# Where the fp32r operands of a 2048-wide two-block network lie modulo 256 bytes, on one core

## The reference

```
# first block
proj = rmsnorm(x) @ w_in                      # 2048 -> q k v o z i f u v_g z_g
y_m  = mlstm(conv(q), conv(k), v, gates) -> norm * sigmoid(o) * silu(z)   # 8 heads of 256
y_g  = gelu(u) * (tril(w_spatial) @ layernorm(gelu(v_g)) + b) * silu(z_g) # 8 heads of 256 ("SGU")
h    = rmsnorm(x + concat(y_m, y_g) @ w_out)
# second block: 16 meta tokens in front (528 rows), 2 layers of
h = layer_norm(alpha * h + concat(conv, attention, rg_lru)(h @ w_in_2) @ w_out_2)
```

## Time and profile before

| | us |
|---|---|
| median of 3 runs | 3194.05 (3190.58 to 3195.36) |
| the profiled execution, its own time | 3189.83 |
| its span in the trace | 3188.3 |
| TensorE (PE) busy | 3127.2, 98% of the span |
| VectorE (DVE) busy | 2205.0, 69% |
| ScalarE (ACT) busy | 1548.3, 49% |
| mean granted TensorE clock | 0.996 of full speed |

### The profile page before, as it was taken

How to read it: one execution, slowest core, us unless ns; L and a number is a source line. 1 busy time by engine, 2 the same in 40 slices (tenths; PEclk the granted TensorE clock), 3 DMA queues, 4 the chain that set the end, 5 groups by cost and what they waited for, 6 DMA issues and landing times.

```text
span 3188.3 us, 59876 instructions
## 1 busy us (share of the span) xinstructions
PE 3127.2 (98%) x23182; PEld 2929.1 (92%) x23182; DVE 2205.0 (69%) x2929; ACT 1548.3 (49%) x2506; POOL 334.4 (10%) x343
## 2 busy tenths in 40 slices
PE   8999999999999999999989999999999999999998
PEld 6899999999999998898889999999998888888898
DVE  7678888888888888876775656656457456556535
ACT  5355555555555556442263655556226455545421
POOL 1000000000000000000000341350000124313000
PEclk9999999999999999999999999999999999999999
DMA  6234444434434345453334222223324322222432
GB/s 208 89 96 106 113 112 112 126 92 112 113 98 118 93 118 178 121 160 106 106 117 135 62 73 81 81 75 106 113 94 151 103 79 80 80 74 68 165 97 90
DMA packets 461728, 342.81 MB, mean 108 GB/s; under 512 B 20504, under 2 KB 451544, under 8 KB 458352
## 3 DMA queue, kind: packets, MB, share of 16 engines
q1 hardware_dynamic: 443712, 296.28, 32.3%
q0 software_dynamic: 8304, 26.92, 2.4%
q10 hardware_dynamic: 9552, 17.37, 1.6%
HBM read 315.04 MB, written 25.46 MB: 107 GB/s over the span
## 4 chain that ended last, share of the span: by engine, by line
PE 82%; DVE 6%; DMA 4%; DVEq 3%; issue 2%; ACT 2%; SPq 0%; ACTq 0%
PE ps L756 13%; PE ps L757 13%; PE ps L758 13%; PE ps L926 8%; PE ps L929 8%; PE ps L928 8%; DMA w_raw_blocks<-in_w_in 3%; PE ps L1179 2%; PE ps L1340 1%; PE ps L1342 1%; PE ps L1338 1%; PE ps L762 1%; PE ps L996 1%; PE ps L764 1%; PE ps L763 1%
## 5 line engine op out<-in xcount | busy, mean ns | idle before, releaser
L756 PE MATMUL ps<-x_high,w_high 128*128 128x264 f32 (+3 forms) x2880 | 913.7, 317 | 19.7 <-DVE x_low L2590 10.7
L757 PE MATMUL ps<-x_low,w_high 128*128 128x264 f32 (+3 forms) x2880 | 882.6, 306 | 0.0
L758 PE MATMUL ps<-x_high,w_low 128*128 128x264 f32 (+3 forms) x2880 | 880.9, 306 | 0.0
L2101 DVE TENSOR_TENSOR w_low<-w_raw,w_high 128x1024 fp32r<-128x1024 f32 x308 | 377.8, 1233 | 330.2 <-ACT w_high L1380 315.0
L756 PEld LDWEIGHTS ps<-x_high,w_high 128*128 128x128 f32 x2880 | 544.1, 189 | 52.1 <-issue 22.4
L757 PEld LDWEIGHTS ps<-x_low,w_high 128*128 128x128 f32 x2880 | 544.3, 189 | 28.0 <-issue 3.3
L758 PEld LDWEIGHTS ps<-x_high,w_low 128*128 128x128 f32 x2880 | 542.5, 188 | 24.8
L926 PE MATMUL ps<-x_high_rows,w_high_blocks 128*128 128x256 f32 x1792 | 507.5, 283 | 4.2 <-DVE u_gelu L2224 2.9
L928 PE MATMUL ps<-x_low_rows,w_high_blocks 128*128 128x256 f32 x1792 | 498.8, 278 | 0.0
L929 PE MATMUL ps<-x_high_rows,w_low_blocks 128*128 128x256 f32 x1792 | 498.8, 278 | 0.0
L1380 ACT ACTIVATE w_high<-w_raw 128x1024 fp32r<-128x1024 f32 x308 | 324.7, 1056 | 277.3 <-PE ps L758 202.4
(11 more groups left out here) (523 smaller groups left out, 5328.5 us busy)
## 6 DMA issues: line engine op xcount, KB each, us to landing
w_raw_blocks<-in_w_in SPq DMA_DIRECT2D x200, 512.0 KB, 5.0
w_raw<-in_w_in SPq DMA_DIRECT2D x384, 256.0 KB, 3.1
w_raw<-in_w_out SPq DMA_DIRECT2D x224, 256.0 KB, 3.0
w_raw_blocks<-in_w_out SPq DMA_DIRECT2D x24, 512.0 KB, 5.6
residual<-residual_stream ACTq DMA_DIRECT2D x8, 1056.0 KB, 10.4
residual_stream<-y_layer ACTq DMA_DIRECT2D x2, 2176.0 KB, 11.6
x_natural<-in_x SPq DMA_DIRECT2D x4, 1024.0 KB, 9.4
x_feature_major<-x_stage POOLq DMA_DIRECT2D x4, 1024.0 KB, 7.9
```

Of the source, the lines that this page charges most:

```text
L756: pe.matmul(dst, wh[:, j, kt, wc], x_hi[:, k, tok], start=first, stop=False)
L757: pe.matmul(dst, wh[:, j, kt, wc], x_lo[:, k, tok], start=False, stop=False)
L758: return pe.matmul(dst, wl[:, j, kt, wc], x_hi[:, k, tok], start=False, stop=last)
L2101: dve.tensor_tensor(wl[:, j], raw[:, j], f(wh[:, j]), ALU.subtract).then_inc(lo_ready, 1)
```

## The change

Offsets alone. `placed(at, residue)` gives the next offset with that residue modulo 256. The activations' rows go from 64 to 128, S2 (and with it `big`) to 32, S1 to 96, S3 to 192, and S3 of the output stage to 160. The regions behind them move along: `work` and `shared` from 64 to 192, the tensors of the second block that start at `big` by -32 bytes and those at `work2` by +128 bytes. The weights, `x_high` and `x_low` of the layers stay where they are. No instruction is added, removed or moved in any engine's order, and the sizes and patterns of all operands are the same. The diff:

```diff
-        ROWS_AT = 64
-        big = r0.at + (ROWS_AT - r0.at) % 256
-        x1_at = [at_ + (ROWS_AT - at_) % 256 for at_ in (xh_at, xl_at)]
+        def placed(at_, residue):
+            return at_ + (residue - at_) % 256
+
+        R_X, R_S2, R_S1, R_S3, R_S3_OUT = 128, 32, 96, 192, 160
+        big = placed(r0.at, R_S2)
+        x1_at = [placed(at_, R_X) for at_ in (xh_at, xl_at)]
...
-        ym_at = big + KT * S * 4
+        ym_at = big + KT * S * 4 + 64
...
-        work = ym_at + KT * S * 4
+        work = ym_at + KT * S * 4 + 96
...
-        for n, name in ((B_S2, "s2"), (B_S1, "s1"), (B_S3, "s3")):
+        for n, name, residue in ((B_S2, "s2", R_S2), (B_S1, "s1", R_S1), (B_S3, "s3", R_S3)):
+            rx_.at = placed(rx_.at, residue)
...
-        rs = Region(big + 6 * BLOCK)
+        rs = Region(rx_.at)
...
-        work2 = r2.at
+        work2 = r2.at + 160
...
-        S3G = big + 77824
+        S3G = placed(rn.at + BLOCK, R_S3_OUT)
```

## The result

| | before | after |
|---|---|---|
| median of 5 runs each, us | 3190.58 (3187.54 to 3195.36) | 3207.67 (3207.1 to 3208.05) |
| profiled execution, its own time | 3189.83 | 3207.67 |
| span in the trace | 3188.3 | 3206.2 |

The ratio is 1.005, with a 95% interval of 1.0036 to 1.0065. The change makes the kernel slower, by 17 us between these medians (by the ratio 16 us, with an interval of 11 to 21). The kernel before has a spread of several us, and its median over 25 to 29 runs each in the later experiments is 3191.66 to 3193.49, so the cost is nearer to 14 to 17 us. The forecast was 9 us faster. The time lies inside the range of 3171 to 3209 only because the range took in rival 3, whose case it is.

What follows compares the result with a forecast made beforehand. TensorE was taken as the bound, busy 3127.2 of 3188.3 us, so time is matmul count times distance. The terms, 0 - 9.0 + 0 + 0, gave -9 us against the 3194.05 us median: 3185 us, range 3171 to 3209.

Steps and rivals of the forecast that it cites:

- rival 3: All block products go slow, since changing residues may prevent the fast pace: +15 to +18 us, 3209 to 3212; chance 0.28.
- two paces exist at one residue: Block products of 256 columns run at 113.3 or 117.8 ns per matmul, 4.45 ns apart, and a stream keeps its pace.
- no other engine is touched: VectorE, ScalarE and the DMAs keep sizes and patterns; their new places were costed at 0.
- the layers stay put: In the layers only small operands move, the split activations and weights don't; cost 0.
- The shares of slow block products: Slow matmuls today, from mean records: 80% in the mLSTM heads, 29% in the SGU heads, 20% in the output stage.
- The value I take: In the mLSTM heads, residue steps cut the slow share from 80% to 29%: -11.2 us before the path discount.
- the token units: Their 384 matmuls, at 279 ns mean record, could go to 276 or 281: -1.2 to +0.8 us, taken as 0.
- The path share: In the mLSTM heads VectorE's chain covers 20%, so 80% of the gain counts: -9.0 us instead of -11.2.
- The whole-row units: First heads and output product: 576 matmuls of 512 columns with activations at 128, -1.2 to +2.3 us, taken as 0.
- Rival 2: Residue doesn't decide; the moment a stream starts behind a hook or wait sets the pace: 3194 us within 0.2%, chance 0.20.
- Rival 1: All block products go fast at 113.3 ns, each step restoring that pace: 17 to 22.6 us gained, 3171 to 3177; chance 0.20.

Runs made afterwards that it cites:

- Experiment 8: Kernel before (all moving operands of the block products at residue 64) with S2 alone at 128: 3192.28 us, ratio 0.9995.
- experiment 9: Kernel before, all residues at 64, with two taps of each q and k convolution left out, so another result is computed: 3184.8 us, ratio 0.998.
- experiment 10: Kernel before with S2 at 128 and two taps of each q and k convolution left out, so another result is computed: 3180.29 us, ratio 0.9965.
- experiment 1: Changed kernel with the activations back at residue 64, the sums left at their new places: 3194.28 us, ratio 1.0003 to the kernel before.
- experiment 2: Changed kernel with all sums back at residue 64, the activations left at 128: 3199.03 us, ratio 1.0022 to the kernel before.
- experiment 5: Changed kernel with all moving operands of the block products at residue 128, like the weights: 3213.27 us, ratio 1.0059 to the kernel before.
- experiment 4: Changed kernel with weights moved to residue 192 and all moving operands of the block products at 128: 3194.57 us, ratio 1.0007 to the kernel before.
- experiment 3: Changed kernel with other residues: activations 0, S2 224, S1 160, S3 64, S3 of the output stage 96: 3203.46 us in one run.
- experiment 7: Kernel before (all at residue 64) with S3 alone at 160, S3 of the output stage still at 64: 3193.45 us, ratio 1.0001.

## Why the prediction was wrong, point by point

**What held.** That TensorE's distances carry the time, that two paces exist at one residue and a stream keeps its pace, their size (4.45 ns), that no other engine is touched (VectorE +1.4 us busy, ScalarE +2.4), and that the layers stay put (-0.8 us for all behind the output product). The shares of slow block products were read somewhat too high: by the last twelve distances of each they are 72% in the mLSTM heads and 22% in the SGU heads, against 80% and 29%.

**The step that failed: "The value I take".** I let the new residues keep the two paces of 64 and only re-deal the shares, from 80% slow to 29% in the mLSTM heads. In fact a residue brings its own paces. At 128, the weights' own residue, it is 120.0 ns, outside the bounds of 113.3 to 117.8 that I had called steady; and at the other new residues the fast one is missing but for two block products of S3. Instead of the term of -11.2 us, all block products together measured +29.5: 1053.2 us inside them became 1082.6. Between them and elsewhere 11.6 us went away: 4.7 in the SGU heads, 4.3 from the mLSTM heads to the output blocks, 2.1 before the first block product and some in the layers. The rest is the 17.9 us by which the span grew. What should have warned me stood in the rows: 256 columns under ever-changing residues at 282 ns, and the token units, difference +64, at 279. S3 at 192 has that very difference, and ran at the very pace (117.7) of those units. I used both rows for rival 3 only, and set a hope against them that no row supported.

**The path share.** Only 20% of a gain in the mLSTM heads was to be lost to VectorE's chain. Experiment 8 won 6.9 us there and got 0; experiments 9 and 10 show why. The chain's length on one stretch is not the share it takes: VectorE's chain sets the time of one matmul in each head, and heads start 88.6 us apart on average in the kernel before and in experiment 8 alike. A gain of TensorE's in this stage was given back whole. Had the forecast mechanism worked, the time would most likely not have moved. In the other direction the wait absorbed 3.4 of the 12.0 us.

**The whole-row units.** I bounded them by mean records, -1.2 to +2.3 us, and with the token units -2.4 to +3.1. The distances moved by more: 233.3 to 227.0 ns for 512 columns is -3.6 us for 576 matmuls, 117.8 to 120.0 for the 384 of the token units +0.8. The two stretches that hold them became 2.1 and 0.8 us shorter, -2.9 together, just outside the bound.

**Rival 3** named the right side and nearly the right price (+15 to +18 on 3194, so 3209 to 3212; measured 3207.67) by a partly wrong road, and that its price was so near is luck: no pace above 117.8 was in it, so the block products cost 29.5 us and not 17.9, and where it let 3 us be swallowed, 11.6 went away. It also blamed the steps between residues. Experiments 1, 2 and 5 show that the steps don't make the changed kernel slow, and can even help. **Rival 2** (the residue doesn't decide) is wrong by experiments 4 and 5, though right in that entry behind a hook picks between the paces of one residue. **Rival 1** needed the fast pace at five new residues; only two block products at one of them had it.

**What stays open**: what in a stream's start picks 113.3 or 117.8 at difference -64, and let two block products at +64 run at 113.3; by what mechanism the difference acts, since the runs show only that it does; and whether rows of the layers, padded so that their residue no longer steps with k, would run faster, which wasn't tried.

## What to carry to other kernels

Where fp32r matmuls stream back to back, read the distance of starts, and treat the addresses of both operands as a setting: here 64 bytes on one side are worth up to 6% of a matmul, what counts is the difference between stationary and moving operand, and equal residues were among the worst of eight for 256 columns and the best of four for 512. Bound an unseen setting by rows with the same difference, also from other code paths, before assuming that it behaves like the present one. And before counting a faster TensorE as a gain, look at the second engine: a stage with a few microseconds of waits for it may have no more to give.

## What was not expected of the hardware

- Difference 0: 120.0 ns for 256 columns, 227 for 512. Difference -64: 113.3 or 117.8, and 233.3. The order turns round with the length of the stream.
- Stepping from difference 0 to -64 without a gap led into the fast pace in 180 of 180 cases, with the first block product at 114.2 ns. From +32 it did so in 78 of 83, from +64 in 12 of 34 (experiments 1, 3 and 7).
- Without step or gap, 328 of 328 block products of the kernel before kept the pace of the one ahead of them.
- Kernels whose paces are fixed seem to have steadier times: five runs of the changed kernel lie within 0.95 us, ten of experiment 2 within 2.2, five of the kernel before, with its two paces, within 7.8. That the choice of pace makes the spread is not shown, as only one execution of each was profiled.
